# Last layer: the four query units in two pairs of seven block products, and ScalarE squaring the expanded keys

## The chip, the core and the metric

The kernel runs on one core of a Trainium2 chip. TensorE multiplies matrices, VectorE and GpSimd do elementwise work, ScalarE computes activations and copies, and SyncE issues the DMAs. The metric is the device time of one launch in microseconds, as the median of several runs. All arithmetic is in float32.

## The reference

A sequence of 256 tokens with 1024 features passes a first block (a gated delta mixer, a mixture of experts, a small extra gate) and then two layers. The change touches only the last of these, which is attention with an index that chooses 64 keys per query:

```
def odd_layer(x, g_norm, w_in, g_kv, w_uk, w_uv, g_q, g_k, w_out, rel_bias):
    xn = rmsnorm(x, g_norm)
    q, ckv, qi, ki, wi, z = _split(xn @ w_in, ODD_SPLITS)   # q: 256 x 1024, 16 heads of 64
    q = rmsnorm(q.reshape(hd), g_q)
    ckv = rmsnorm(ckv, g_kv)
    k = rmsnorm((ckv @ w_uk).reshape(hd), g_k)
    v = (ckv @ w_uv).reshape(hd)
    ...
        score = einsum('bqh,bqhs->bqs', wib, relu(einsum('bqhd,bsd->bqhs', qib, ki)))
        _, idx = lax.top_k(score, top_k)                     # causal, 64 of 256
        logits = einsum('bqhd,bqkhd->bqhk', qb, ksel) * 64 ** -0.5 + bias
        probs = softmax(logits)
        out = einsum('bqhk,bqkhd->bqhd', probs, vsel)
    return x + (out * silu(z)) @ w_out
```

## The kernel before

Each engine has its own program, written out in order in `odd_tensor`, `odd_scalar`, `odd_vector`, `odd_gpsimd` and `odd_sync`; what binds them are semaphores. An engine never overtakes a waiting instruction of its own. Weights arrive in units of 1024 rows by 256 columns (1 MB) in slots; slots 0 to 3 hold the four query units, slots 4 and 5 the two expansions (keys, values). `xt` holds the input turned, features on the partitions.

TensorE's order in this layer (`odd_tensor`): the index queries (L3776), bias rows, index keys (L3784), the compressed rows (L3793), the index scores (L3803). Then the stretch that the change rewrites (the calls from L3949 on): `queries(0)`, the turning of the compressed rows (L320), `queries(1)`, `query_sums(0)`, `expand(4, 0)` and `expand(4, 1)` (the keys, L3834), `queries(2)`, `query_sums(1)`, `queries(3)`, `query_sums(2)`, the turning of the keys by `turn_tensor` (L320), `query_sums(3)`, `expand(5, 0)` (the values), `logits(0)`, `expand(5, 1)`, `logits(1)`, `gates(0)` (L3846). From there on gates, logits, weights and values alternate until the output product (L3944).

One `queries(i)` is 16 matmuls of a 128x128 weight tile on 256 tokens (L3815); in the trace each float32 matmul has two records. The result stands in bank 2 or 3, features on the partitions. ScalarE's `keep_queries` copies it out, scaled, into `qT` (L4041) and squares it (L4042); `query_sums` adds the squares of each head by a matmul (L3825). ScalarE's `expand` copies the expanded keys out (L4047).

VectorE (`odd_vector`) makes the choice of keys: for each half t of the queries it weighs the scores (L4143, L4145), then finds the 64 largest in eight steps of MAX8 and MATCH_REPLACE8 (L4152, L4153), and writes the mask (L4155). After both halves it squares the expanded keys (L4161), adds the squares (L4162), and scales the keys by their norms, one instruction for each half of the tokens (L4165), for which ScalarE computes Ln and Exp (L4091, L4093). GpSimd adds the mask to the bias, four instructions for each half (L4347), each half from the moment that its mask is there.

## Time and profile before

| | |
|---|---|
| median of 3 runs | 1010.59 us (1009.43 to 1010.63) |
| profiled execution, its own time | 1010.96 us |
| its span in the trace | 1009.6 us |
| TensorE busy | 964.8 us (96%) |
| VectorE busy | 556.2 us (55%) |
| ScalarE busy | 335.3 us (33%) |
| GpSimd busy | 52.5 us (5%) |

The span is the time from the first to the last instruction in the trace; the launch takes 1.4 us more. The table says that TensorE is nearly always busy; where it isn't, and which stretch another engine decides, only the rows by time say. In a row of a timeline, the first number is the start in us from the beginning of the span, the second the time that the group of instructions took, and the bracket at the end how long the engine was idle before it and which instruction ended that.

### The profile page before, as it was taken

To read this page: it belongs to the slowest core of one execution; us is meant where nothing else is said; L and a number is where in the kernel's file an instruction comes from. 1 tells how busy PE (TensorE), PEld (TensorE's weight loads), DVE (VectorE), ACT (ScalarE), POOL (GpSimd) and SP (SyncE) were. 2 spreads that over 40 slices of the span, in tenths; PEclk is the share of its full clock that TensorE was granted. 3 is DMA by queue.
4 is the path that set the end of the run, shared out by engine and by line. 5 is a ranking of instruction groups with operands and counts; after the bars stand their busy time and mean duration, and the time that the engine had idled before them with its cause. 6 is when DMAs were issued, how large, how long until landed. Compare 5 with 4: busy or idle time off the path is not lost.

```text
span 1009.6 us, 21951 instructions
## 1 busy us (share of the span) xinstructions
PE 964.8 (96%) x9305; PEld 750.0 (74%) x9305; DVE 556.2 (55%) x1192; ACT 335.3 (33%) x904; POOL 52.5 (5%) x81
## 2 busy tenths in 40 slices
PE   9999999999999999799877999999999999999998
PEld 6788888888887794344322589988888988877887
DVE  3976876876868233111100496875555465194675
ACT  2455557556545222001100223132111321233550
POOL 1111011011000000000000000000000000034000
PEclk9999999999999999899987999999999999999999
DMA  8213215134156999999999934442555344652221
GB/s 347 87 65 133 102 65 178 56 136 180 45 187 268 423 372 354 423 429 427 436 429 411 407 162 149 169 176 90 186 182 179 127 168 167 185 192 84 84 84 43
DMA packets 34311, 211.63 MB, mean 210 GB/s; under 512 B 4432, under 2 KB 8976, under 8 KB 15904
## 3 DMA queue, kind: packets, MB, share of 16 engines
q1 hardware_dynamic: 33920, 210.13, 54.0%
q8 instruction: 76, 1.25, 0.5%
q14 instruction: 27, 0.22, 0.1%
q10 hardware_dynamic: 288, 0.03, 0.0%
HBM read 209.03 MB, written 1.11 MB: 208 GB/s over the span
## 4 chain that ended last, share of the span: by engine, by line
PE 81%; DMA 7%; DVE 4%; SPq 3%; issue 2%; ACT 2%; POOL 0%; DVEq 0%; ACTq 0%; POOLq 0%
PE ps L558 11%; PE ps L3174 9%; PE ps L3074 5%; DMA slots<-in_w 5%; PE ps L584 5%; PE ps L2036 3%; PE ps L3846 3%; PE ps L2920 3%; PE ps L3815 3%; SPq L1922 3%; PE ps L3944 2%; PE ps L970 2%; PE ps L3214 2%; PE ps L2684 2%; PE ps L2007 2%
## 5 line engine op out<-in xcount | busy, mean ns | idle before, releaser
L558 PE MATMUL ps<-xt,slots 128*128 128x256 f32 x512 | 122.3, 384 | 0.0
L558 PEld LDWEIGHTS ps<-xt,slots 128*128 128x128 f32 x512 | 93.8, 190 | 12.8 <-issue 0.4
L1308 DVE SCALAR_TENSOR_TENSOR arena<-arena 128x256 f32<-128x256 f32 x128 | 56.6, 501 | 0.0
L2036 PE MATMUL ps<-arena 128*32 128x512 f32 x224 | 47.5, 639 | 6.7 <-DMA arena<-in_w 6.1
L2378 DVE TENSOR_TENSOR arena<-arena,ps 128x256 f32<-128x256 f32 x8 | 3.4, 421 | 87.9 <-ACT arena L2168 87.9
L2036 PE MATMUL ps<-slots,arena 128*32 128x512 f32 x192 | 47.6, 641 | 2.4 <-DMA xt<-in_wu 2.4
L4347 POOL TENSOR_TENSOR arena<-arena 128x512 f32<-128x512 f32 (+1 forms) x8 | 17.8, 2262 | 597.3 <-DVE arena L4155 597.3
L2168 ACT ACTIVATE arena<-ps 128x256 f32<-128x256 f32 x8 | 3.1, 384 | 111.6 <-PE ps L2036 111.6
L970 PE MATMUL ps<-slots,yt 128*128 128x256 f32 x128 | 30.3, 396 | 2.1 <-DMA slots<-in_wu 2.1
L2036 PEld LDWEIGHTS ps<-arena 128*32 128x32 f32 x224 | 11.9, 117 | 26.4 <-issue 19.3
L3846 PE MATMUL ps<-xt,slots 128*128 128x256 f32 x128 | 30.6, 385 | 0.6 <-ACT arena L4047 0.6
L2007 PE MATMUL ps<-arena,x 128*128 128x128 f32 x256 | 30.4, 276 | 0.1
L2007 PEld LDWEIGHTS ps<-arena,x 128*128 128x128 f32 x256 | 29.3, 192 | 1.3 <-issue 0.8
L3174 PE MATMUL ps<-slots,yt 128*128 128x256 f32 x128 | 30.2, 379 | 0.0
L3174 PE MATMUL ps<-extra,arena 128*128 128x256 f32 x128 | 30.2, 379 | 0.0
L3174 PE MATMUL ps<-slots,arena 128*128 128x256 f32 x128 | 30.2, 379 | 0.0
L970 PEld LDWEIGHTS ps<-slots,yt 128*128 128x128 f32 x128 | 24.9, 197 | 6.0 <-issue 2.5
L3815 PE MATMUL ps<-xt,slots 128*128 128x256 f32 x128 | 28.5, 380 | 0.0
L2388 DVE COPY arena<-ps 128x512 f32<-128x512 f32 x7 | 4.8, 692 | 40.8 <-PE ps L2076 40.8
L3815 PEld LDWEIGHTS ps<-xt,slots 128*128 128x128 f32 x128 | 24.1, 190 | 3.9 <-issue 0.8
L3846 PEld LDWEIGHTS ps<-xt,slots 128*128 128x128 f32 x128 | 23.2, 190 | 4.9 <-issue 2.0
L3174 PEld LDWEIGHTS ps<-extra,arena 128*128 128x128 f32 x128 | 24.3, 190 | 3.3
(590 smaller groups left out, 2178.8 us busy)
## 6 DMA issues: line engine op xcount, KB each, us to landing
slots<-in_wu SPq DMA_DIRECT2D x90, 1024.0 KB, 5.7
arena<-in_wu SPq DMA_DIRECT2D x20, 1024.0 KB, 12.9
arena<-in_w SPq DMA_DIRECT2D x5, 4096.0 KB, 27.9
slots<-in_w SPq DMA_DIRECT2D x8, 2048.0 KB, 33.0
extra<-in_w SPq DMA_DIRECT2D x2, 4096.0 KB, 28.6
yt<-in_w SPq DMA_DIRECT2D x3, 2048.0 KB, 29.4
extra<-in_wu SPq DMA_DIRECT2D x4, 1024.0 KB, 19.7
xt<-in_wu SPq DMA_DIRECT2D x4, 1024.0 KB, 30.3
```

The source lines that it names most:

```text
L558: q = M.matmul(bank(b, T), self.slots[:, s, k, n * P:(n + 1) * P], self.xt[:, k, :], start=(k == 0), stop=(k == KT - 1))
L584: q = M.matmul(bank(b, UC), rows[:, k, :], weights[:, k, :], start=(k == 0), stop=(k == HK - 1))
L970: q = M.matmul(self.out_bank(t, cg), self.yt[:, KT + k, t * P:(t + 1) * P], self.slots[:, s, k, :], start=(k == 0 and (cg % 2 == 0 or (t, ...
L1308: q = V.scalar_tensor_tensor(g.cn[:, s], src, w, g.cn[:, s], ALU.mult, ALU.add)
L1922: SP.dma_start(part(self.flat(s)), part(I["wu"][U_MOE + u].rearrange("p a b -> p (a b)"))).then_inc(*(self.lands(s) if b else g.low_in.up()))
L2007: q = M.matmul(g.gathered_in(i, k), self.x[:, t, k * P:(k + 1) * P], g.sb[:, t].rearrange("p e s -> p (e s)"), start=(t == 0), stop=(t == ...
L2036: q = M.matmul(self.ps[r, 2, :], g.xg[:, half * (KT // 2) + k, r], self.flat(slots[e])[:, k * 512:(k + 1) * 512], start=(half == 0 and k = ...
L2920: q = M.matmul(into[:, n * P:(n + 1) * P], w[:, k, n * P:(n + 1) * P], x[:, k, :], start=(n == 0 and k == 0 and not more), stop=(k == HK - ...
L3074: q = M.matmul(into[n], rows[:, k, :], weights[:, k, :], start=(h == 1 and k == 0 and n in (1, 5, 6, 7)), stop=(h == 0 and k == HK - 1), s ...
L3174: q = M.matmul(into, rows[:, k, :], weights[:, k, :], start=(k == 0 and not more), stop=(k == HK - 1), skip_group_check=True)
L3815: q = M.matmul(bank(2 + i % 2, T, n * T), self.slots[:, i, k, n * P:(n + 1) * P], self.xt[:, k, :], start=(k == 0), stop=(k == KT - 1), sk ...
L3846: q = M.matmul(bank(g.z_banks[u], T, n * T), self.slots[:, u, k, n * P:(n + 1) * P], self.xt[:, k, :], start=(n == 0 and k == 0), stop=(k ...
```

## The change

The product of queries is a product of two matrices. Two units side by side (slots 0 and 1, then 2 and 3) are cut in two by rows and in two by units, and the tokens in two halves, so that a pair of units is a 2x2 by 2x2 block product. It is made from seven block products in place of eight, by sums and differences of blocks made beforehand and folds made afterwards. One block product is 8 matmuls of a 128x128 tile on 128 tokens. `query_product(p, n)` is product n (1, 7, 2, 6, 5, 4, 3 in this order) of pair p. Products 2, 4 and 3 add onto what 1, 7 and 5 have left in banks 0, 3 and 2; before that ScalarE has to copy product 1 (`keep_query_first`) and VectorE has to use 7 and 5.

VectorE gets: four operations on the token blocks (`mix_query_rows`, 128x512: y11-y21, s1=y21+y22, s2=s1-y11, y12-s2, with y for blocks of `xt`), four on the weights of each pair (`mix_queries`, 128x1024: t1=b12-b11, b22-b12 in place of b12, t2=b22-t1, t4=b21-t2, with b for blocks of the two slots), and five folds for each pair (`fold_queries`, 256 elements a partition). The folds are numbered through: `q_folds` 1 to 5 for the first pair, 6 to 10 for the second. Folds 1 and 2 of the first pair stand between the two searches, 3 to 5 behind the weighing of the second half; folds 6 and 7 stand between the two scalings of the keys, 8 to 10 behind them.

ScalarE scales and squares the queries in three parts for each pair (`keep_query`), two of them from `qT` in SBUF. It squares the expanded keys out of the banks itself (in `expand`), and VectorE's squaring (L4161) goes. On TensorE the query sums stand together in pairs, and the turning of the keys is parted: two turns ahead of `expand(5, 0)`, two behind.

```diff
+        def query_product(p, n):
+            a, b = 2 * p, 2 * p + 1
+            one, two, rows, xt = self.slots[:, a], self.slots[:, b], g.q_rows, self.xt
+            t1, t2, t4 = g.q_mixes[p]
+            if n == 1:
+                g.q_in.append([self.landing(s) for s in (a, b)])
+                M.wait_ge(*g.q_in[p][0])
+                if p == 0:
+                    M.wait_ge(*g.rrow_kept(1))
+                else:
+                    M.wait_ge(*g.expand_kept(1))
+            elif n == 7:
+                M.wait_ge(*g.q_rows_made(1))
+                M.wait_ge(*g.q_mix(4 * p + 2))
+                if p > 0:
+                    M.wait_ge(*g.q_folds(5))
+            elif n == 2:
+                M.wait_ge(*g.q_first(p + 1))
+            elif n == 6:
+                M.wait_ge(*g.q_rows_made(3))
+                M.wait_ge(*g.q_mix(4 * p + 3))
+            elif n == 5:
+                M.wait_ge(*g.q_mix(4 * p + 1))
+            elif n == 4:
+                M.wait_ge(*g.q_mix(4 * p + 4))
+                M.wait_ge(*g.q_folds(5 * p + 2))
+            else:
+                M.wait_ge(*g.q_in[p][1])
+                M.wait_ge(*g.q_rows_made(4))
+                M.wait_ge(*g.q_folds(5 * p + 3))
+            into = bank({1: 0, 2: 0, 6: 1, 5: 2, 3: 2, 7: 3, 4: 3}[n], T)
+            x, w = {1: (xt[:, 0:HK, 0:P], one[:, 0:HK]), 2: (xt[:, HK:KT, 0:P], one[:, HK:KT]), 6: (rows[:, 1], t2),
+                    7: (rows[:, 2], two[:, 0:HK]), 5: (rows[:, 0], t1), 4: (xt[:, HK:KT, P:2 * P], t4),
+                    3: (rows[:, 3], two[:, HK:KT])}[n]
+            for f in range(2):
+                for k in range(HK):
+                    q = M.matmul(into[:, f * P:(f + 1) * P], w[:, k, f * P:(f + 1) * P], x[:, k, :],
+                                 start=(f == 0 and k == 0 and n not in (2, 3, 4)), stop=(k == HK - 1),
+                                 skip_group_check=True)
+            if n == 4:
+                q.then_inc(*self.multiplied[a].up())
+            elif n == 3:
+                q.then_inc(*self.multiplied[b].up())
+                g.q_pair_done.append([self.multiplied[s].last() for s in (a, b)])
...
-        queries(0)
+        for n in (1, 7, 2, 6):
+            query_product(0, n)
         M.wait_ge(*g.relu(2))
         M.wait_ge(*g.c_norm(1))
         self.turn_tensor(g.ck, 2, [4], g.c_turned, g.c_cols)
-        queries(1)
-        query_sums(0)
+        for n in (5, 4, 3):
+            query_product(0, n)
         M.wait_ge(*g.c_cols(1))
         M.wait_ge(*self.landing(4))
         expand(4, 0)
         expand(4, 1)
-        queries(2)
+        query_sums(0)
         query_sums(1)
-        queries(3)
-        query_sums(2)
+        for n in (1, 7, 2, 6, 5, 4, 3):
+            query_product(1, n)
         M.wait_ge(*g.expand_kept(2))
         M.wait_ge(*g.scaled(1))
-        self.turn_tensor(g.kk, KT, [4, 5], g.k_turned, g.k_kept)
-        query_sums(3)
+        turn_keys(0)
+        turn_keys(1)
+        M.wait_ge(*g.q_folds(10))
         M.wait_ge(*self.landing(5))
         expand(5, 0)
+        turn_keys(2)
+        turn_keys(3)
+        query_sums(2)
+        query_sums(3)
         logits(0)
...
+        def keep_query_first(p):
+            A.wait_ge(*g.q_of(p, 1))
+            if p > 0:
+                A.wait_ge(*g.q_folds(5))
+            A.activation(g.q_sums_of[0], bank(0, T), ACT.Copy).then_inc(*g.q_first.up())
+        def keep_query(p, part):
+            a, scale = 4 * p, g.feat[:, F_Q:F_Q + 1]
+            if part == 0:
+                A.wait_ge(*g.q_of(p, 2))
+                at, src = (slice(a, a + 2), slice(0, P)), bank(0, T).rearrange("p (n t) -> p n t", n=2)
+            elif part == 1:
+                A.wait_ge(*g.q_folds(5 * p + 4))
+                at = (slice(a, a + 4), slice(P, T))
+            else:
+                A.wait_ge(*g.q_folds(5 * p + 5))
+                at = (slice(a + 2, a + 4), slice(0, P))
+            if part > 0:
+                src = g.qT[:, at[0], at[1]]
+            A.activation(g.q_squares[:, at[0], at[1]], src, ACT.Square).then_inc(*g.q_squared.up())
+            if part > 0:
+                A.wait_ge(*g.q_squared.last())
+            q = A.activation(g.qT[:, at[0], at[1]], src, ACT.Copy, scale=scale)
+            if part == 2:
+                q.then_inc(*g.q_kept.up())
...
+            if s == 4:
+                A.activation(halves(g.pq[:, 0, t]), self.ps[:, b0:b0 + 2], ACT.Square)
+            A.activation(halves(dst[:, t]), self.ps[:, b0:b0 + 2], ACT.Copy).then_inc(*g.expand_kept.up())
...
-        keep_queries(0)
+        keep_query_first(0)
+        keep_query(0, 0)
         self.turn_scalar(g.ckt, 2, [4], g.c_turned, g.c_cols, g.fcol(F_KV))
-        keep_queries(1)
+        keep_query(0, 1)
+        keep_query(0, 2)
         expand(4, 0, g.kk)
         expand(4, 1, g.kk)
-        keep_queries(2)
+        keep_query_first(1)
         A.wait_ge(*g.squares(1))
         A.activation(g.sh[:, :, :], g.sh[:, :, :], ACT.Ln, scale=1.0 / CD, bias=self.col(0)).then_inc(*g.s_ln.up())
         A.wait_ge(*g.s_ln(1))
         A.activation(g.sh[:, :, :], g.sh[:, :, :], ACT.Exp, scale=-0.5).then_inc(*g.s_exp.up())
-        keep_queries(3)
-        self.turn_scalar(g.kT, KT, [4, 5], g.k_turned, g.k_kept, lambda k: g.feat[:, F_K:F_K + 1])
+        keep_query(1, 0)
+        turn_keys(0)
+        turn_keys(1)
+        keep_query(1, 1)
+        keep_query(1, 2)
+        expand(5, 0, g.vv)
+        turn_keys(2)
+        turn_keys(3)
         A.wait_ge(*g.q_sums(4))
...
+        def fold_queries(p, n):
+            u1, u2, u3 = g.q_sums_of
+            first, second, third, fourth = (bank(m, T) for m in range(4))
+            pair = lambda a: a.rearrange("p (n t) -> p n t", n=2)
+            low, high = (g.qT[:, 4 * p + 2 * m:4 * p + 2 * m + 2, :] for m in range(2))
+            if n == 0:
+                V.wait_ge(*g.q_first(p + 1))
+                V.wait_ge(*g.q_of(p, 6))
+                o = V.tensor_tensor(u2, u1, second, ALU.add)
+            elif n == 1:
+                V.wait_ge(*g.q_folds(5 * p + 1))
+                o = V.tensor_tensor(u3, u2, fourth, ALU.add)
+            elif n == 2:
+                V.wait_ge(*g.q_of(p, 5))
+                V.wait_ge(*g.q_folds(5 * p + 2))
+                o = V.tensor_tensor(high[:, :, P:T], pair(u3), pair(third), ALU.add)
+            elif n == 3:
+                V.wait_ge(*g.q_pair_done[p][0])
+                o = V.tensor_tensor(low[:, :, P:T], pair(u2), pair(fourth), ALU.add)
+            else:
+                V.wait_ge(*g.q_pair_done[p][1])
+                o = V.tensor_tensor(high[:, :, 0:P], pair(u2), pair(third), ALU.add)
+            o.then_inc(*g.q_folds.up())
...
+        mix_query_rows()
+        mix_queries(0)
         V.wait_ge(*g.index_kept(1))
         V.wait_ge(*g.r_spread(1))
         V.tensor_tensor(g.kit[:, :], g.kit[:, :], bank(0, T), ALU.mult).then_inc(*g.kit_made.up())
+        mix_queries(1)
         for t in range(NT):
             S = (t + 1) * P
             V.wait_ge(*g.wi_kept(t + 1))
...
                     v(q)
             q.then_inc(*g.masked.up())
             V.wait_ge(*g.masked(2 * t + 1))
+            if t > 0:
+                for n in (2, 3, 4):
+                    fold_queries(0, n)
             v(V.tensor_tensor(wk, mk, g.late[:, t, 0:S], ALU.subtract))
             for r in range(SEL // 8):
                 v(V.max(g.best[:, :], wk))
                 v(V.match_replace(wk, g.best[:, :], wk, TAKEN))
             v(V.tensor_scalar(wk, wk, TAKEN / 2, -BIG, ALU.is_gt, ALU.mult))
             V.tensor_tensor(mk, wk, g.late[:, t, 0:S], ALU.subtract).then_inc(*g.masked.up())
+            if t == 0:
+                fold_queries(0, 0)
+                fold_queries(0, 1)
 
         byh = lambda x: x.rearrange("p (h d) -> p h d", h=CH)
         squares = g.pq[:, 0].rearrange("p t (h d) -> p t h d", h=CH)
         V.wait_ge(*g.expand_kept(2))
         keys = g.kk[:, :, :].rearrange("p t (h d) -> p t h d", h=CH)
-        v(V.tensor_tensor(squares, keys, keys, ALU.mult))
         V.tensor_reduce(g.sh[:, :, :], squares, AX, ALU.add).then_inc(*g.squares.up())
         V.wait_ge(*g.s_exp(1))
         for t in range(NT):
             q = V.tensor_tensor(keys[:, t], keys[:, t], g.sh[:, t].unsqueeze(2).to_broadcast([P, CH, CD]), ALU.mult)
+            if t == 0:
+                fold_queries(1, 0)
+                fold_queries(1, 1)
         q.then_inc(*g.scaled.up())
+        for n in (2, 3, 4):
+            fold_queries(1, n)
```

On TensorE, from the index scores to the second pair, this stands before (the last column is the shape of the result, then the number of matmuls):

```order
L3803 MATMUL ps<-arena 128x256 x4
L3815 MATMUL ps<-xt,slots 128x256 x16
L320 MATMUL ps<-cst,arena 128x128 x4
L3815 MATMUL ps<-xt,slots 128x256 x16
L3825 MATMUL ps<-cst,arena 128x2 x4
L3834 MATMUL ps<-slots,arena 128x512 x8
L3815 MATMUL ps<-xt,slots 128x256 x16
L3825 MATMUL ps<-cst,arena 128x2 x4
L3815 MATMUL ps<-xt,slots 128x256 x16
L3825 MATMUL ps<-cst,arena 128x2 x4
L320 MATMUL ps<-cst,arena 128x128 x16
```

and this after, where L3857 is `query_product` (the first four rows are products 1, 7, 2, 6 of pair 0), L3892 the expansion and L3883 the query sums:

```order
L3814 MATMUL ps<-arena 128x256 x4
L3857 MATMUL ps<-xt,slots 128x128 x8
L3857 MATMUL ps<-arena,slots 128x128 x8
L3857 MATMUL ps<-xt,slots 128x128 x8
L3857 MATMUL ps<-arena 128x128 x8
L320 MATMUL ps<-cst,arena 128x128 x4
L3857 MATMUL ps<-arena 128x128 x8
L3857 MATMUL ps<-xt,arena 128x128 x8
L3857 MATMUL ps<-arena,slots 128x128 x8
L3892 MATMUL ps<-slots,arena 128x512 x8
L3883 MATMUL ps<-cst,arena 128x2 x8
L3857 MATMUL ps<-xt,slots 128x128 x8
```

Both query units of the first pair now stand ahead of the expansion of the keys in 56 small matmuls in place of 32 large ones, and the query sums of the first pair behind it.

On VectorE, between the end of the first search and the second one, this stands before:

```order
L4154 TENSOR_SCALAR arena<-arena 128x128
L4155 TENSOR_TENSOR arena<-arena 128x128
L4143 TENSOR_SCALAR arena<-arena 128x256
L4145 SCALAR_TENSOR_TENSOR arena<-arena 128x256 x3
L4150 TENSOR_TENSOR arena<-arena 128x256
L4152 MAX arena<-arena 128x8
```

and this after (L4273 to L4286 are folds 1 to 5 of the first pair):

```order
L4314 TENSOR_SCALAR arena<-arena 128x128
L4315 TENSOR_TENSOR arena<-arena 128x128
L4273 TENSOR_TENSOR arena<-arena,ps 128x256
L4276 TENSOR_TENSOR arena<-arena,ps 128x256
L4300 TENSOR_SCALAR arena<-arena 128x256
L4302 SCALAR_TENSOR_TENSOR arena<-arena 128x256 x3
L4280 TENSOR_TENSOR yt<-arena,ps 128x2x128
L4283 TENSOR_TENSOR yt<-arena,ps 128x2x128
L4286 TENSOR_TENSOR yt<-arena,ps 128x2x128
L4310 TENSOR_TENSOR arena<-arena 128x256
L4312 MAX arena<-arena 128x8
```

Two folds have come ahead of the weighing of the second half and three behind it, ahead of its search.

## Rows read from the trace of the kernel before

**Rows 1.** Chain of waits, last layer: start us, us, what.
```profile
883.59 7.10 PE ps L3815 x32
890.70 0.44 PE ps L320 x4
891.13 6.91 PE ps L3815 x32
898.04 0.79 PE ps L3825 x8
898.83 6.97 PE ps L3834 x16
...
921.30 0.51 PE ps L320 x4
...
921.83 1.58 ACT yt L334 x4
...
923.45 0.66 PE ps L320 x4
...
932.75 1.03 ACT arena L4047
...
933.92 5.42 PE ps L3846 x24
```

**Rows 2.** TensorE by time, layer before: start us, us, engine, line, operation, count.
```profile
642.39 1.95 PE L2920 MATMUL ps<-arena,slots 128*128 128x128 f32 x16
644.17 1.95 PE L2920 MATMUL ps<-yt,slots 128*128 128x128 f32 x16
```

**Rows 3.** ScalarE by time, last layer.
```profile
888.12 0.91 ACT L4035 ACTIVATE arena<-arena 128x256 f32<-128x256 f32 x2
...
898.08 0.69 ACT L4041 ACTIVATE yt<-ps,arena 128x512 f32<-128x512 f32 x1 [5.44 <-PE ps L3815]
898.67 0.59 ACT L4042 ACTIVATE arena<-ps 128x512 f32<-128x512 f32 x1
...
921.83 3.15 ACT L334 ACTIVATE yt<-ps,arena 128x256 f32<-128x256 f32 x8
```

**Rows 4.** VectorE by time, layer before.
```profile
642.59 0.42 DVE L3400 TENSOR_TENSOR arena<-arena,ps 128x256 f32<-128x256 f32 x1 [0.23 <-PE ps L2920]
...
645.85 1.22 DVE L3376 TENSOR_TENSOR arena<-slots,arena 128x1024 f32<-128x1024 f32 x1
```

**Rows 5.** VectorE by time, last layer, before the first search.
```profile
874.82 0.42 DVE L4137 TENSOR_TENSOR arena<-arena,ps 128x256 f32<-128x256 f32 x1 [7.58 <-ACT arena L4004]
883.65 0.29 DVE L4143 TENSOR_SCALAR arena<-arena 128x128 f32<-128x128 f32 x1 [8.41 <-ACT arena L4020]
```

**Rows 6.** DMA queue by time, then DMA issues: KB each, median us to landing.
```profile
859.79 2.05 SPq L276 DMA_DIRECT2D slots<-in_wu  x2
...
slots<-in_wu SPq DMA_DIRECT2D x2, 1024.0 KB, 6.0
```

**Rows 7.** VectorE and then GpSimd by time, last layer.
```profile
892.08 4.24 DVE L4145 SCALAR_TENSOR_TENSOR arena<-arena 128x256 f32<-128x256 f32 x3
...
906.90 4.09 DVE L4161 TENSOR_TENSOR arena<-arena 128x2048 f32<-128x2048 f32 x1 [0.49 <-ACT arena L4047]
911.02 2.29 DVE L4162 TENSOR_REDUCE arena<-arena 128x32 f32<-128x2048 f32 x1
914.43 5.47 DVE L4165 TENSOR_TENSOR arena<-arena 128x1024 f32<-128x1024 f32 x2 [1.12 <-ACT arena L4093]
...
891.92 5.52 POOL L4347 TENSOR_TENSOR arena<-arena 128x512 f32<-128x512 f32 x4 [588.24 <-DVE arena L4155]
906.48 12.33 POOL L4347 TENSOR_TENSOR arena<-arena 128x1024 f32<-128x1024 f32 x4 [9.04 <-DVE arena L4155]
```

**Rows 8.** TensorE by time, experts; then busy us by window, the granted clock behind POOL.
```profile
494.49 0.62 PE L2036 MATMUL ps<-slots,arena 128*32 128x512 f32 x2 [2.39 <-DMA xt<-in_wu]
...
496.00:497.00 1.00, 1.00 (x8) 0.27 (x4) 0.00 (x0) 0.00 (x0) 0.00 (x0) 0.50 0.91 393
```

More of the change, by code:

```diff
@@ L3805, in odd_tensor @@
             q.then_inc(*g.scores.up())
-        g.q_done, g.z_done = [], []
-        def queries(i):
-            M.wait_ge(*self.landing(i))
-            if i > 1:
-                M.wait_ge(*g.q_kept(i - 1))
-            for n in range(2):
-                for k in range(KT):
-                    q = M.matmul(bank(2 + i % 2, T, n * T), self.slots[:, i, k, n * P:(n + 1) * P], self.xt[:, k, :],
-                                 start=(k == 0), stop=(k == KT - 1), skip_group_check=True)
-            q.then_inc(*self.multiplied[i].up())
-            g.q_done.append(self.multiplied[i].last())
+        g.q_in, g.q_pair_done, g.z_done = [], [], []
@@ new lines, in odd_tensor @@
+        HK = KT // 2
+        def query_product(p, n):
[43 more added lines that the diff above has]
+            else:
+                q.then_inc(*g.q_products.up())
@@ L3820, in query_sums, with turn_keys @@
+        def turn_keys(j):
+            if j > 1:
+                M.wait_ge(*g.k_kept(j - 1))
+            for f in range(2):
+                for t in range(NT):
+                    q = M.transpose(bank(4 + j % 2, P, (2 * f + t) * P), g.kk[:, t, (2 * j + f) * P:(2 * j + f + 1) * P],
+                                    c["ident"])
+            q.then_inc(*g.k_turned.up())
         def query_sums(i):
-            M.wait_ge(*g.q_kept(i + 1))
+            M.wait_ge(*g.q_kept(i // 2 + 1))
             for n in range(2):
```

51 lines of the change are left out of this document (42 added, 9 removed).

## The prediction

> **What bounds the kernel now.** The table of busy shares comes first: TensorE is busy 96% of the span. That alone would say that fewer matmul columns are less time, so the next view is the chain of waits in the last layer. Up to the gates at 933.92 every piece of it but a few is TensorE's own work [rows 1]: two of the four query blocks (there are four such, 7.10 and 6.91 us in turn) with the turning of the compressed rows between them, the query sums, the expansion of the keys. Two pieces are ScalarE's: 1.58 us in the turning of the keys (921.83) and 1.03 us ahead of the gates (932.75). Behind 933.92 nothing is changed, TensorE works without a wait of its own, and what starts later there ends later. So the whole question is at what time the gates start. The views after that are the timelines of ScalarE, VectorE and GpSimd beside this stretch, since the new products wait for folds and copies on them.
>
> **What it removes.** Four blocks of 7.10 and 6.91 us, twice each, are 28.0 us [rows 1]. In their place come 14 block products of 16 records on 128 columns. The layer before has products of exactly this form: they start 1.78 us apart, and the last result is there 1.95 us after the start [rows 2]. 14 x 1.78 = 24.9 us, so TensorE's own work shrinks by 3.1 us, a ninth and not an eighth. The turning of the keys took from 921.30 to 924.11, 2.8 us, with the wait for ScalarE in it [rows 1]. Parted in two, with the expansion of the values between, it waits for nothing and costs four times 0.44 us (the 4 records at 890.70 [rows 1]), 1.8 us. That is another 1.0 us. Together: -4.1 us. The rest of TensorE's work (turning of the compressed rows, expansions, sums, logits) is the same and only stands in another order.
>
> **VectorE's mixing lies in idle time.** Before the operation at 874.82 it is idle for 7.58 us, and before 883.65 for 8.41 us [rows 5]. The four operations on tokens (half of 1.22 us and a little, 2.6 us) and the four on the first pair of weights (1.22 us each, started some 1.15 us apart [rows 4], 4.7 us) fill 7.3 of the first 7.58 us, the four on the second pair 4.7 of the second 8.41 us. The last two query units are issued from 859.79 on and land 6.0 us after (median), 868 at the latest [rows 6], ahead of both. Should the first set overrun by a microsecond, the operation at 874.82 has until TensorE's scores at 882.0, so I cost it at nothing; were a unit to land 8 us late, the cover would be gone and each microsecond would count.
>
> **The waits that come in**, one by one, with the start of the first product at 883.59:
>
> First wait, product 2. Products 1 and 7 are issued by 883.59 + 3.56 = 887.15. Product 2 adds onto bank 0, which ScalarE must copy first, and ScalarE is in its chain for the compressed rows until 888.12 + 0.91 = 889.03 [rows 3]. The old `keep_queries(0)` also waited for that, but TensorE had 7 us of `queries(0)` to issue meanwhile and now has 3.6. A copy of 256 elements takes 0.39 us (3.15 us for 8 [rows 3]), and TensorE starts 0.14 us after what it waits for (933.92 against 932.75 + 1.03 [rows 1]): product 2 at 889.56. Loss 2.4 us.
>
> Second wait, product 3 of the first pair. Products 2, 6, the turning, 5 and 4 are issued by 889.56 + 4 x 1.78 + 0.44 = 897.12. Fold 1 needs product 6, there at 891.34 + 1.95 = 893.3, though VectorE is free from 891.8 on; folds 1 and 2 at 0.42 us each [rows 4] end at 894.2, the first weighing at 894.5. Then come the three operations at L4145, which took 4.24 us while GpSimd worked from 891.92 to 897.4 [rows 7], 1.41 us each against 0.42 for an operation of this size alone [rows 4]. The same GpSimd work now slows two of them: 894.5 + 2 x 1.4 + 0.5 = 897.8, fold 3 at 898.2, product 3 at 898.35. Loss 1.2 us.
>
> Third wait, product 3 of the second pair. TensorE: 898.35 + 1.78 + 6.97 (keys) + 2 x 0.79 (sums) + 6 x 1.78 = 919.4. VectorE: product 3 is there at 900.3, fold 5 at 900.75. The search took from 896.32 to 906.41 (end of L4145, start of the idle 0.49 us before 906.90 [rows 7]); its first operation had GpSimd beside it and now hasn't, so I take 9.2 us: 909.95. The squaring of 4.09 us is gone, which is why this isn't worse; the sums take 2.29 [rows 7], ScalarE's Ln and Exp 0.65 (two small ones of about 0.3), the first scaling half of 5.47 [rows 7]: 915.6. Fold 6 waits for product 6, there at 916.0; folds 6 and 7 end at 916.85, the second scaling at 919.6, fold 8 at 920.0, and product 3 starts at 920.2. Loss 0.8 us.
>
> Fourth wait, logits. TensorE: 920.2 + 1.78 + 2 x 0.44 + 3.54 (the later expansion is half of 6.97 and a little) + 2 x 0.44 + 2 x 0.79 = 928.85. ScalarE: it turns out the first keys by 924.2, then squares and scales the last query parts (0.59 and 0.69 [rows 3], then about 0.4 and 0.4, with two waits on itself: 2.3 us), copies the values (1.03 [rows 1]) and turns out the other keys (4 x 0.39 [rows 3]): 929.1. Loss 0.4 us.
>
> **The sum.** -3.1 - 1.0 + 2.4 + 1.2 + 0.8 + 0.4 = +0.7; with some 0.1 for the first matmuls behind a wait, +0.8 us. The profiled execution took 1010.96 us (span 1009.6) and would take 1011.8; the median is 0.37 us lower, which is within the scatter of the three runs, so the forecast is 1010.59 + 0.8 = 1011.4 us.
>
> **What the trace of before doesn't show.** (a) How much GpSimd slows the weighing and the scalings in their new places: at best not at all (0.42 and 1.22 us), which takes 1.9 us from the second and third wait together and gives -1.1 in all; at worst every one as now, +1.5. I take the middle since the same GpSimd work stands there. (b) Folds while GpSimd works: 0.42 us each if they run as [rows 4], 1.41 us each if they are slowed as L4145 is; I take 0.42, because the sums of squares at 911.02, with one operand, kept to 2.29 us beside GpSimd [rows 7]. (c) The clock after the first wait: below.
>
> That VectorE and GpSimd hinder each other stands in rows 7. The Trainium skill (GPSIMD Engine Reference, Specifications) says that this happens with VectorE instructions with two inputs in SBUF or in a two-port mode. A fold has one input in the banks, so by that rule it is not slowed and the sum stays.
>
> **Rivals.**
>
> *The clock falls in the first wait.* TensorE is without work from 887.3 to 889.56, 2.3 us. Among the experts it was idle for 2.39 us before 494.49, and the granted clock at 496 was 0.50, which is 1.2 in place of 2.4 GHz [rows 8]. For it: nearly the same idle time. Against it: among the experts only a small part of the array worked (128*32 in that row), here TensorE works in full on both sides of the wait. Between half of product 2 and both products 2 and 6 would run at half speed, 0.9 to 3.6 us longer; I take 1.7. The weighing then starts later and meets less of GpSimd's work, so that 0.7 to 1.2 us remain: 1012.3 us.
>
> The Trainium skill (TensorE: Matmul & The Clock Gate, Why this matters for your kernels) warns of idle gaps above some 3 us. By that this wait would be free and the sum would stay at 1011.4; the 2.39 us of rows 8 speak against it.
>
> *The folds are slowed by GpSimd* (slower). GpSimd works on the second mask for 12.3 us [rows 7], from 909.9 on, so folds 6, 7 and 8 are all beside it, and folds 1 and 2 beside the first mask. Each fold between product 6 and the freeing of its bank is on TensorE's path. At 1.41 us each, 1.0 us more, times five, and the search shifted too: some +5 to +7 us, 1016 to 1018. It decides from 0.6 us a fold on, where the five cost 1 us more and the kernel is slower by 2. For it: rows 7. Against it: the one-operand sums.
>
> *The waits are shorter than reckoned* (faster). If the weighings run alone and ScalarE copies product 1 in between, the 4.1 us are kept to 3: 1007.8. Against it: ScalarE's order is fixed, and 889.03 is a measured time. The likelier form is -1 us by (a): 1009.5, no change.
>
> *It doesn't do what it says:* a pair's mixes late by a landing, so that scores start late. Rows 6 leave 2 us at least; 1014.
>
> **Chances.** What a measurement of this kernel can tell from no change is about 0.2%, 2.0 us. Forecast with the clock kept 0.45 (1011.4), with the clock down 0.25 (1012.3), waits shorter 0.15 (1009.5, a third of it below 1008.6), folds slowed 0.11 (mostly above 1012.6), late mixes or something else 0.04. From these: faster 0.05, same 0.79, slower 0.16 (0.10 of the folds, 0.03 of the clock with more slowing, 0.03 others). The range 1009.3 to 1013.4 takes in both ends of (a) with the clock down, and leaves out the folds' 1016 and the 1007.8.
>
> **What would show it.** Product rows 1.78 us apart: the first term. TensorE idle for about 2.3 us ahead of product 2, released by ScalarE; about 1 us ahead of each product 3, released by VectorE; the gates' start near 934.7 (933.92 before). A granted clock of 0.50 behind this wait is the first rival. Folds of over 0.6 us are the second. A start of the scores later than 882.0 means that the mixing wasn't hidden. The forecast is wrong if the gates start before 932.7 or after 936.

## The result, and the profile after

The changed kernel took 1012.09 us (median of 17 runs, 1010.58 to 1014.02), against 1010.59 us for the kernel before on the same chip (17 runs, 1009.08 to 1012.13). The ratio is 1.0016, with a 95% interval of 1.0009 to 1.0024: slower by 1.6 us (1.5 between the medians), within the 0.2% that were called no change, and 0.7 us above the forecast of 1011.4.

The forecast was made at the start of the gates, so the comparison begins there. "Stretch" below is the time from the start of the first query product to the start of the gates. It leaves out what differs between two executions further up: TensorE's clock falls among the experts in every profile of this study, not always at the same places, and the stretch starts anywhere from 881.5 to 883.5 us. Before, it began at 883.52 by TensorE's timeline (the chain has 883.59) and ended at 933.92 [rows 1], 50.40 us:

```profile
883.52 7.17 PE L3815 MATMUL ps<-xt,slots 128*128 128x256 f32 x32
```

After, it is TensorE's timeline below (start, time taken, engine, line, operation, tiles, shape; in the bracket the idle time before and what ended it; the last line of such a view counts only the records up to the time at which the view stops):

```profile
880.56 1.58 PE L3814 MATMUL ps<-arena 64*128 64x128 f32 x16 [0.68 <-issue]
882.07 2.05 PE L3857 MATMUL ps<-xt,slots 128*128 128x128 f32 x16
...
887.90 3.68 PE L3857 MATMUL ps<-xt,slots 128*128 128x128 f32 x16 [1.99 <-ACT arena L4106]
891.40 1.97 PE L3857 MATMUL ps<-arena 128*128 128x128 f32 x16
...
895.42 1.95 PE L3857 MATMUL ps<-xt,arena 128*128 128x128 f32 x16
897.74 2.02 PE L3857 MATMUL ps<-arena,slots 128*128 128x128 f32 x16 [0.36 <-DVE yt L4280]
...
918.97 1.95 PE L3857 MATMUL ps<-arena,slots 128*128 128x128 f32 x16
...
921.63 3.60 PE L3892 MATMUL ps<-slots,arena 128*128 128x512 f32 x8
925.07 1.04 PE L3874 MATMUL ps<-cst,arena 128*128 128x128 f32 x8
925.94 1.84 PE L3883 MATMUL ps<-cst,arena 128*128 128x2 f32 x16
927.89 0.72 PE L3921 MATMUL ps<-yt 64*128 64x128 f32 x8
928.54 5.40 PE L3892 MATMUL ps<-slots,arena 128*128 128x512 f32 x8
933.87 0.71 PE L3921 MATMUL ps<-yt 64*128 64x128 f32 x8
935.14 2.18 PE L3904 MATMUL ps<-xt,slots 128*128 128x256 f32 x9 [0.56 <-ACT arena L4135]
```

The reader is to see three things. Products run 1.78 us apart (1.86 to 1.89 behind a wait or another kind of work), and the wait for ScalarE's copy ahead of product 2 is there (1.99 us idle, 2.16 us from the time at which it could have been issued). Two groups take nearly twice their time: product 2 with 3.68 us in place of 2.05, and the later expansion of the values (L3892) with 5.40 us, where the same form took 3.60 at 921.63. And no wait stands ahead of the second pair's product 3 at 918.97. The stretch is 882.07 to 935.14, 53.07 us, 2.67 longer than before.

The view by windows says what slowed the two groups (bounds, length, busy time with the count for PE, PEld, DVE, ACT, POOL; then the granted clock, the DMA share and GB/s):

```profile
886.00:888.00 2.00, 0.10 (x1) 0.10 (x1) 1.79 (x9) 1.78 (x6) 0.00 (x0) 1.00 0.99 418
888.00:890.00 2.00, 2.00 (x10) 2.00 (x11) 1.83 (x9) 0.00 (x0) 0.00 (x0) 0.50 0.41 172
890.00:892.00 2.00, 2.00 (x14) 2.00 (x14) 0.29 (x1) 0.38 (x2) 1.53 (x2) 0.64 0.00 0
...
929.00:931.00 2.00, 2.00 (x4) 0.79 (x3) 1.69 (x6) 0.00 (x0) 0.00 (x0) 0.50 0.00 0
931.00:933.00 2.00, 2.00 (x5) 0.82 (x4) 0.00 (x0) 0.00 (x0) 0.00 (x0) 0.65 0.00 0
```

The granted clock was 0.50, the lower of TensorE's two levels (1.2 in place of 2.4 GHz), behind the first wait and again behind the query sums and logits. In the profile of before it stayed at 1.00 through the whole stretch:

```profile
883.50:934.00 50.50, 49.37 (x231) 37.03 (x230) 35.59 (x75) 17.70 (x43) 17.85 (x8) 1.00 0.39 138
```

VectorE's side (columns as in TensorE's timeline), with the mixing first, then the first pair's folds, then the second's:

```profile
865.71 0.69 DVE L4244 TENSOR_TENSOR arena<-xt 128x512 f32<-128x512 f32 x1
...
871.89 1.23 DVE L4262 TENSOR_TENSOR arena<-slots,arena 128x1024 f32<-128x1024 f32 x1
873.37 0.42 DVE L4293 TENSOR_TENSOR arena<-arena,ps 128x256 f32<-128x256 f32 x1 [0.25 <-ACT arena L4067]
...
893.47 0.42 DVE L4273 TENSOR_TENSOR arena<-arena,ps 128x256 f32<-128x256 f32 x1 [3.15 <-PE ps L3857]
...
894.27 1.31 DVE L4300 TENSOR_SCALAR arena<-arena 128x256 f32<-128x256 f32 x1
895.61 1.53 DVE L4302 SCALAR_TENSOR_TENSOR arena<-arena 128x256 f32<-128x256 f32 x3
897.17 0.42 DVE L4280 TENSOR_TENSOR yt<-arena,ps 128x256 f32<-128x256 f32 x1
...
912.08 2.99 DVE L4327 TENSOR_TENSOR arena<-arena 128x1024 f32<-128x1024 f32 x1 [0.65 <-ACT arena L4190]
...
916.46 1.91 DVE L4327 TENSOR_TENSOR arena<-arena 128x1024 f32<-128x1024 f32 x1
918.29 0.41 DVE L4280 TENSOR_TENSOR yt<-arena,ps 128x256 f32<-128x256 f32 x1
```

After the mixing VectorE still waits 0.25 us for ScalarE where it was idle for 7.58 us [rows 5]: the cover was just wide enough. Every fold takes 0.42 us, those beside GpSimd too, which worked on the second mask from 909.31 on:

```profile
909.31 11.28 POOL L4514 TENSOR_TENSOR arena<-arena 128x1024 f32<-128x1024 f32 x4 [13.89 <-DVE arena L4315]
```

### The profile page after: what moved, and what is told of

The parts are those of the page before. It is cut to its first block, busy times and chain, and to the rows that moved or that the text cites. A ratio compares the mean times of both kernels' runs of the same rounds, so it can differ in the third digit from the quotient of the medians.

```text
span 1010.8 us, 22188 instructions
## 1 busy us (share of the span) xinstructions
PE 963.5 (95%) x9401; PEld 753.0 (74%) x9401; DVE 564.4 (56%) x1213; ACT 339.4 (34%) x912; POOL 51.1 (5%) x81
## 4 chain that ended last, share of the span: by engine, by line
PE 81%; DMA 6%; DVE 5%; SPq 3%; ACT 2%; issue 2%; POOL 0%; DVEq 0%; ACTq 0%; POOLq 0%
PE ps L558 11%; PE ps L3174 9%; PE ps L3074 5%; PE ps L584 5%; DMA arena<-in_w 4%; PE ps L2036 4%; PE ps L3904 3%; PE ps L2920 3%; SPq L1922 2%; PE ps L4002 2%; PE ps L970 2%; PE ps L3214 2%; PE ps L2007 2%; PE ps L3857 2%; PE ps L2684 2%
## 5 line engine op out<-in xcount | busy, mean ns | idle before, releaser
L558 PE MATMUL ps<-xt,slots 128*128 128x256 f32 x512 | 122.3, 384 | 0.0
L558 PEld LDWEIGHTS ps<-xt,slots 128*128 128x128 f32 x512 | 93.8, 190 | 12.8 <-issue 0.4
L2036 PE MATMUL ps<-slots,arena 128*32 128x512 f32 x192 | 45.1, 613 | 1.0 <-DMA xt<-in_wu 0.8
L3904 PE MATMUL ps<-xt,slots 128*128 128x256 f32 x128 | 30.6, 385 | 0.6 <-ACT arena L4135 0.6
L970 PEld LDWEIGHTS ps<-slots,yt 128*128 128x128 f32 x128 | 23.9, 190 | 5.6 <-issue 2.6
L3904 PEld LDWEIGHTS ps<-xt,slots 128*128 128x128 f32 x128 | 23.2, 190 | 4.9 <-issue 2.0
L3174 PEld LDWEIGHTS ps<-slots,arena 128*128 128x128 f32 x128 | 24.3, 190 | 3.3
L3174 PEld LDWEIGHTS ps<-slots,yt 128*128 128x128 f32 x128 | 24.2, 190 | 3.3
```

Of the source, the lines that this page charges most:

```text
L558: q = M.matmul(bank(b, T), self.slots[:, s, k, n * P:(n + 1) * P], self.xt[:, k, :], start=(k == 0), stop=(k == KT - 1))
L970: q = M.matmul(self.out_bank(t, cg), self.yt[:, KT + k, t * P:(t + 1) * P], self.slots[:, s, k, :], start=(k == 0 and (cg % 2 == 0 or (t, ...
L2036: q = M.matmul(self.ps[r, 2, :], g.xg[:, half * (KT // 2) + k, r], self.flat(slots[e])[:, k * 512:(k + 1) * 512], start=(half == 0 and k = ...
L3174: q = M.matmul(into, rows[:, k, :], weights[:, k, :], start=(k == 0 and not more), stop=(k == HK - 1), skip_group_check=True)
L3904: q = M.matmul(bank(g.z_banks[u], T, n * T), self.slots[:, u, k, n * P:(n + 1) * P], self.xt[:, k, :], start=(n == 0 and k == 0), stop=(k ...
```

## The experiments

Theory A: the change would be even or a little slower by its waits, and what it lost beyond that are the two clock falls. Theory B: the loss is in the waits and in VectorE's added work themselves; the clock only shows it.

**The first wait filled.** Five matmuls of 256 columns, whose result isn't used, stand in the wait.

```diff
-        for n in (1, 7, 2, 6):
+        for n in (1, 7):
+            query_product(0, n)
+        for k in range(5):
+            M.matmul(bank(1, T), self.slots[:, 0, k, 0:P], self.xt[:, k, :], start=(k == 0), stop=(k == 4),
+                     skip_group_check=True)
+        for n in (2, 6):
             query_product(0, n)
```

> The changed kernel with five more matmuls of 256 columns (2.2 us) between products 7 and 2 of the first pair, into a bank that product 6 then overwrites: the wait for ScalarE stays where it is, but TensorE works through it. Theory A (half of the loss is the clock that falls behind this wait): no granted clock of 0.50 behind 887, products 2 and 6 take 3.6 us together and not 5.5, the gates start 0.7 to 1.7 us earlier after the start of the first product than the 53.1 us of the changed kernel, ratio to the kernel before 1.0005 to 1.001. Theory B (the waits alone cost the time, the clock is made up for by the later wait of product 3): ratio stays 1.0016.

Measured: ratio to before 0.9999 (0.999 to 1.0008), 1010.53 us. TensorE around the filler and at the end of the stretch:

```profile
887.08 2.32 PE L4009 MATMUL ps<-xt,slots 128*128 128x256 f32 x10
889.24 2.05 PE L3857 MATMUL ps<-xt,slots 128*128 128x128 f32 x16
...
898.42 1.80 PE L3857 MATMUL ps<-arena,slots 128*128 128x128 f32 x14 [1.33 <-DVE yt L4285]
...
928.58 0.71 PE L3921 MATMUL ps<-yt 64*128 64x128 f32 x8
929.22 3.70 PE L3892 MATMUL ps<-slots,arena 128*128 128x512 f32 x8
932.85 0.72 PE L3921 MATMUL ps<-yt 64*128 64x128 f32 x8
934.13 3.04 PE L3904 MATMUL ps<-xt,slots 128*128 128x256 f32 x13 [0.56 <-ACT arena L4140]
```

Product 2 starts at the same distance from the first product as before the filling (5.83 us), but takes 2.05 us, and the clock falls nowhere in this layer. The stretch is 50.72 us, 0.32 more than the kernel before and 2.35 less than the changed one. So the waits and the added work cost what the forecast's sum gave, nearly, and the rest was the clock. It also shows that the first fall hangs on TensorE being idle, not on what stands behind the wait. The ratio came out below theory A's 1.0005 to 1.001, and the stretch gained 2.35 us in place of 0.7 to 1.7, because the second fall was missing too. That isn't the filler's doing as far as is shown: two kernels below are without the second fall though nothing there was changed.

**The waits taken away.** Products in the order 1, 7, 6, 5, 2, 4, 3, and fold 3 (which product 3 waits for) right behind folds 1 and 2, ahead of the second half's weighing.

```diff
-        for n in (1, 7, 2, 6):
+        for n in (1, 7, 6, 5, 2):
             query_product(0, n)
...
-        for n in (5, 4, 3):
+        for n in (4, 3):
             query_product(0, n)
...
             if t > 0:
-                for n in (2, 3, 4):
+                for n in (3, 4):
                     fold_queries(0, n)
...
                 fold_queries(0, 1)
+                fold_queries(0, 2)
```

(The second pair likewise.)

> The changed kernel with the products in the order 1, 7, 6, 5, 2, 4, 3 in both pairs, and the third fold of each pair beside the first two (between the searches; between the scalings). Theory A (the loss is the wait for ScalarE's copy of product 1, the clock behind it and product 3's wait for the fold): TensorE has 7.1 us of products before it needs the copy, none of these waits is left, the first pair ends 2.5 to 3.5 us earlier, ratio to the kernel before 0.997 to 0.999 (1007.5 to 1009.5 us). Theory B (VectorE's chain of weighing, search, sums and scaling sets the gates' start in the end): the gain goes into a wait of product 3 of the second pair or of the keys' turning for VectorE, and the ratio is 0.9995 to 1.001.

Measured: 0.9957 (0.9943 to 0.997), 1006.26 us. TensorE from the first product:

```profile
883.42 2.05 PE L3857 MATMUL ps<-xt,slots 128*128 128x128 f32 x16
885.31 1.95 PE L3857 MATMUL ps<-arena,slots 128*128 128x128 f32 x16
887.09 3.74 PE L3857 MATMUL ps<-arena 128*128 128x128 f32 x32
890.67 1.95 PE L3857 MATMUL ps<-xt,slots 128*128 128x128 f32 x16
892.45 0.60 PE L320 MATMUL ps<-cst,arena 128*128 128x128 f32 x4
892.89 1.95 PE L3857 MATMUL ps<-xt,arena 128*128 128x128 f32 x16
894.68 1.95 PE L3857 MATMUL ps<-arena,slots 128*128 128x128 f32 x16
...
925.49 5.39 PE L3892 MATMUL ps<-slots,arena 128*128 128x512 f32 x8
```

No bracket is left among the products. The stretch is 48.68 us, with one fall in it (the expansion at 925.49); without that fall, which costs 5.39 - 3.70 = 1.7 us, it would be 47.0, 3.7 us below the filled kernel, where the two waits that are gone measure 2.16 and 1.50 us. The same 14 products that made the kernel slower by 1.6 us make it faster by 4.3 us (3.0 to 5.8) once nothing is waited for. This version beats both kernels, and by more than theory A's 0.997 to 0.999.

**Only fold 3 put back** behind the weighing, with the new order of the products kept.

```diff
-                for n in (3, 4):
+                for n in (2, 3, 4):
                     fold_queries(0, n)
```

(In the second pair likewise.)

> The order 1, 7, 6, 5, 2, 4, 3 with the folds where the changed kernel has them. Theory A (the order alone takes away the wait for ScalarE, but fold 3 then lies behind the weighing of the second half, which GpSimd slows): product 3 of the first pair waits 1 to 2.5 us for fold 3, ratio 0.997 to 0.9985, stretch 49.5 to 50.5 us without a fall of the clock. Theory B (the place of the folds doesn't matter since VectorE is ahead): ratio 0.9957 as with the early fold.

Measured: 1.0016 (1.0004 to 1.0028), 1011.85 us. VectorE, then TensorE:

```profile
890.44 0.87 DVE L4300 TENSOR_SCALAR arena<-arena 128x256 f32<-128x256 f32 x1
891.35 4.20 DVE L4302 SCALAR_TENSOR_TENSOR arena<-arena 128x256 f32<-128x256 f32 x3
895.58 0.42 DVE L4280 TENSOR_TENSOR yt<-arena,ps 128x256 f32<-128x256 f32 x1
```

```profile
896.14 3.65 PE L3857 MATMUL ps<-arena,slots 128*128 128x128 f32 x16 [3.25 <-DVE yt L4280]
```

The whole gain is gone; the stretch is 52.00 us. Fold 3 stands behind a weighing that GpSimd slows to 4.20 us, as in [rows 7], product 3 waits 3.25 us, and the clock falls behind that wait too (3.65 us for a product in place of 1.95). Theory A named the right cause but priced it too low: it had a wait of 1 to 2.5 us, no fall, and a ratio of 0.997 to 0.9985. In the second pair product 3 doesn't wait, so it is the place of one operation of 0.42 us in the first pair that decides between 1006 and 1012 us.

**The narrow matmuls parted.** In the kernel with its first wait unfilled, half of `expand(5, 0)` goes between the turning of the keys and the query sums, and ScalarE copies the values later.

```diff
-        expand(5, 0)
+        expand(5, 0, (0,))
         turn_keys(2)
         turn_keys(3)
+        expand(5, 0, (1,))
         query_sums(2)
```

> The changed kernel with the first expansion of the values cut in its two halves of 1.7 us, the later two turnings of the keys between them, and ScalarE's copy of the values behind the turned keys. Theory A (the clock fell at 929 because query sums of 2 columns, a short wait and logits on 64 rows follow each other with too little work in them): with one turning less beside them the fall becomes rarer, the second expansion of the values takes 3.6 us and not 5.3, ratio 1.0005 to 1.001, if it doesn't fall in the profile. Theory B (the fall at 929 is a matter of one execution, or has another cause): ratio stays 1.0016, and the profile may show it again.

Measured: 1.0007 (0.9998 to 1.0016), 1011.53 us; stretch 51.19 us. The fall behind the first wait is there (at 890.6), the one at the end isn't. With one fall the stretch stands 0.47 us above the filled kernel's and 1.88 below the changed kernel's, so the second fall is the dearer; some 0.2 us of that is the parting itself (see the next run). The timed ratios overlap, so this kernel alone doesn't prove it.

**Both edits together** (new order, early fold 3, parted narrow matmuls).

> The order 1, 7, 6, 5, 2, 4, 3 with the third fold early, and the values' first expansion cut in two with the keys' turnings between. In the profile of the first of these alone the clock fell once more, at 925.5, and the second expansion of the values took 5.4 us instead of 3.7. Theory A (the fall comes of too little work in a row behind the turnings): both together have no fall in this layer, the stretch from the first product to the gates is 47.0 to 47.4 us (48.7 with the order alone), ratio to the kernel before 0.994 to 0.9955. Theory B (cutting the expansion does nothing): a fall again, 48.7 us, ratio as the order alone, 0.9957.

Measured: 0.996 (0.9946 to 0.9974), 1006.82 us; stretch 46.80 us with no fall in it, 1.9 less than with the order alone and 0.2 less than that without its fall. It is 3.6 us below the kernel before, which is what the forecast's first term gives by measured rows (-2.6) with the keys' turning (-1.0): with no wait left, nothing else remains. But the ratio isn't the 0.994 to 0.9955 of theory A: the medians don't differ (1006.26 and 1006.82, five runs each). The profile of the order alone was its slowest execution, 1009.13 us with a mean granted clock of 0.983; the other four took 1005.98 to 1007.10 us with 0.985 to 0.988. One profile is one execution, and its fall is not the rule there.

**Only ScalarE's squares** (the products of before, with the squaring on ScalarE):

```diff
+            if s == 4:
+                A.activation(halves(g.pq[:, 0, t]), self.ps[:, b0:b0 + 2], ACT.Square)
...
-        v(V.tensor_tensor(squares, keys, keys, ALU.mult))
```

(Against the kernel before.)

> The kernel before with one part of the change alone: ScalarE squares the expanded keys from the banks, VectorE's squaring of 4.1 us is left out. Theory A (the keys' scaling wasn't what the turning waited for, it ended 1.4 us ahead of it): ratio 0.9995 to 1.0005. Theory B (GpSimd and VectorE hindered each other there, and what stands behind comes earlier): ratio 0.998 to 0.9995.

Measured: 0.999 (0.998 to 1.0), 1009.62 us; stretch 50.39 against 50.40. GpSimd's second mask and VectorE's scaling get quicker:

```profile
905.37 9.28 POOL L4348 TENSOR_TENSOR arena<-arena 128x1024 f32<-128x1024 f32 x4 [9.04 <-DVE arena L4157]
```

```profile
913.31 3.55 DVE L4166 TENSOR_TENSOR arena<-arena 128x1024 f32<-128x1024 f32 x2 [4.32 <-ACT arena L4095]
```

12.33 us became 9.28 and 5.47 became 3.55 [rows 7]: there is no squaring beside GpSimd any more, and the scaling, which waits for ScalarE until 913.31, overlaps it only up to 914.65. But TensorE's chain sets the end here. The ratio lies in theory B's range, though its interval reaches 1.0; what was quicker didn't come through to the gates, so in the stretch theory A holds. This part of the change frees VectorE for the second pair's folds; alone it moves the stretch by nothing.

**The mixing all but left out.** Every mixing operation works on 4 columns, so the queries aren't the products asked for.

```diff
-            rows = g.q_rows
+            y11, y12, y21, y22 = (y[:, :, 0:4] for y in (y11, y12, y21, y22))
+            rows = g.q_rows[:, :, :, 0:4]
...
+            b11, b21, b12, b22, t1, t2, t4 = (y[:, :, 0:4] for y in (b11, b21, b12, b22, t1, t2, t4))
```

> The changed kernel with VectorE's mixing of tokens and weights reduced to 4 of 128 or 256 columns (the rest of the blocks is left out, so the queries are not the reference's). Theory A (the mixing of 7.5 and 4.9 us lies wholly in time in which VectorE was idle): the scores start as before in relation to the last matmul ahead of them, and the stretch from the first product to the gates is as in the changed kernel for the same falls of the clock, 50.7 us without one, 53.1 with two. Theory B (mixing costs): the stretch or the gap ahead of the scores (0.68 us) is shorter by 0.5 us or more.

Measured: 1010.06 us, one run; stretch 51.39 us with the fall behind the first wait alone, 0.2 from the parted kernel with the same single fall, and what the filled kernel's +0.32 and the first fall's 0.65 (reckoned below) give together: 51.37. The gap ahead of the scores is 0.67 us, 0.68 with the full mixing. The mixing was hidden.

**The narrow matmuls tripled**, in the filled kernel: 16 more matmuls with 2 columns (32 records) ahead of the 8 of the last query sums, to the same result.

```diff
         turn_keys(3)
+        for more in range(2):
+            for i in (2, 3):
+                M.wait_ge(*g.q_kept(2))
+                for n in range(2):
+                    for t in range(NT):
+                        M.matmul(bank(6, 2, t * CH + 4 * i + 2 * n), g.q_squares[:, 2 * i + n, t * P:(t + 1) * P],
+                                 c["columns"][:, 6:8], start=True, stop=True, skip_group_check=True)
         query_sums(2)
```

> The changed kernel with the filled first wait, and the 8 query sums of the second pair (matmuls with 2 columns) made three times over, the first two times for nothing. TensorE is busy in the trace all through. Theory A (matmuls of 2 columns don't keep the clock up): 3.4 us more of them, and a fall of the clock to 0.50 behind them, the second expansion of the values takes 5.3 us and not 3.7; the stretch is 50.7 + 3.4 + 1.7 = 55.8 us. Theory B (what the trace shows as busy keeps the clock up): no fall, stretch 54.1 us.

Measured: 1016.3 us, one run; stretch 57.36 us. The windows:

```profile
928.00:930.00 2.00, 2.00 (x20) 2.00 (x19) 0.00 (x0) 0.00 (x0) 0.00 (x0) 0.94 0.04 8
930.00:932.00 2.00, 2.00 (x14) 1.98 (x14) 0.00 (x0) 0.67 (x3) 0.00 (x0) 0.50 0.00 0
932.00:934.00 2.00, 2.00 (x6) 0.90 (x5) 1.50 (x5) 0.00 (x0) 0.00 (x0) 0.50 0.00 0
934.00:936.00 2.00, 2.00 (x4) 0.81 (x3) 0.48 (x2) 0.00 (x0) 0.00 (x0) 0.50 0.00 0
```

TensorE is busy 2.00 of 2.00 us in each, and still the clock falls to 0.50, for about 6.8 us. The stretch is 6.64 us longer than the filled kernel's, of which 3.50 are the added matmuls; the fall cost the other 3.1, more than the 1.7 of theory A, whose stretch was 55.8.

**The control: as much work, but wide.** In the filled kernel, in the same place, 8 matmuls of 256 columns. This run was on another chip, where the kernel before took 1010.09 us (one run).

```diff
         turn_keys(3)
+        M.wait_ge(*g.q_kept(2))
+        for k in range(8):
+            M.matmul(bank(1, T), self.slots[:, 5, k, 0:P], self.xt[:, k, :], start=(k == 0), stop=(k == 7),
+                     skip_group_check=True)
         query_sums(2)
```

> This is the kernel with the filled first wait, and 8 more matmuls of 256 columns on 128 features stand on TensorE between the turning of the last keys and the query sums; their result is not used. They are the control for the kernel with more narrow matmuls in the same place, whose clock fell for 6.8 us. Theory A (the clock falls in the second place because the cluster of matmuls with 2 columns counts for little): wide matmuls in front leave the same narrow cluster behind them as in the filled kernel, which kept 1.00, so the granted clock stays at 1.00 and the stretch from the start of the first product to the start of the gates is that of the filled kernel and 8 x 0.44 = 3.5 us, 50.7 + 3.5 = 54.2 us. Theory B (any longer stay in this place, or any work put there, brings the fall): a fall to 0.50 behind them, at least 1.7 us more, 56 us or more.

Measured: 1014.47 us, one run; stretch 883.44 to 937.43, 53.99 us against the 54.2 of theory A.

```profile
928.00:930.00 2.00, 2.00 (x11) 1.77 (x10) 0.00 (x0) 0.45 (x2) 0.00 (x0) 1.00 0.00 0
930.00:932.00 2.00, 2.00 (x20) 1.96 (x20) 0.00 (x0) 0.02 (x1) 0.00 (x0) 1.00 0.00 0
932.00:934.00 2.00, 2.00 (x12) 1.16 (x13) 1.15 (x5) 0.65 (x3) 0.00 (x0) 1.00 0.00 0
```

The same 3.5 us of added work brings no fall when it is wide. That speaks for what is multiplied, and against the time spent or the place, as what took the clock. Each of these two is one execution, and falls come and go between executions, so it is strong evidence and no proof; the fall in the narrow one is the longest in this layer of any profile here.

**What the timed runs add.** The record has the mean granted clock of each timed execution, over the whole kernel. It is 0.9832 in the changed kernel (mean of 17 runs) and 0.9854 in the kernel before (27 runs made with the later experiments); the filled kernel has 0.9851, the parted one 0.9841, the late fold 0.9843 (11 runs each), the new order alone and with the parting 0.9860 (5 each). The difference of 0.0022 is 2.2 us of full clock in 1011; in the changed kernel's profile the two falls together take 3.4 us of it (windows of 1 us from 888 to 892 and from 928 to 933). So, as an estimate that takes the falls among the experts as alike in both kernels, a timed execution of the changed kernel loses on average some two thirds of what its profile shows, and one of the new order next to nothing.

## Why the prediction was right, and where not

The time was held by the range, and the main mechanism was the one forecast: gain on TensorE given back in waits. What the clock added on top was foreseen in part, as a rival, and in part not at all. Term by term, with the filled kernel as the one without clock falls:

- **Products, -3.1 us**: measured -2.6. The 14 products took 12.77 and 12.59 us, 25.4 and not 24.9: four of them, each the first behind a wait or another kind of work, held the next up for 1.86 to 1.89 us and not 1.78. **Keys' turning, -1.0**: four times 0.44 us, as reckoned.
- **First wait, +2.4**: 2.16. It came about as described; in the changed kernel ScalarE's chain ended at 886.67 + 0.91 = 887.58, 5.51 us behind the first product, against 5.44 reckoned from [rows 3].
- **Second wait, +1.2**: 1.50 in the filled kernel, 0.54 in the changed one, where TensorE was late already.
- **Third wait, +0.8**: nothing. The second scaling was reckoned at half of 5.47 us and took 1.91, so that in the changed kernel fold 8 ended at 918.70, ahead of 918.97. **Fourth wait, +0.4**: 0.25. From the last query sums to the logits 1.95 us pass, where the first pair's sums pass the engine on after 1.70; ScalarE's last keys are copied at 927.75, and the logits start 0.14 us later, as forecast.
- **The sum, +0.8**: +0.32 without a fall. The waits came to 3.9 us and not 4.8, the products gave back 0.5 less: small errors of both signs.
- **The mixing at nothing**: right (0.25 us of idle time left behind it, and the run almost without it).
- **Rival "the clock falls in the first wait" (0.25)**: it happened in the profile. Product 2 lost 1.61 us by it, and the second wait took 0.96 of that back, so 0.65 us remain; the prediction had said 0.7 to 1.2. It gave this rival 1012.3, which is nearer to the 1012.09 measured than the forecast is. The Trainium skill (TensorE: Matmul & The Clock Gate, Why this matters for your kernels) warns of idle gaps above some 3 us, and by that this wait was free; here 1.99 us were enough, in the profiles of all three kernels that had the wait (changed, parted, mixing left out: falls at 888.0, 890.6 and 888.8, that is 0.1 to 1.4 us after product 2 had started). The prediction gave this case too small a chance against the forecast.
- **What failed**: the step that priced everything behind the first wait at full clock. The later expansion of the values was put at half of 6.97 us, 3.54, and took 5.33 from start to start, 1.70 more than in the filled kernel. 0.32 + 0.65 + 1.70 = 2.67 us, the whole difference of the stretches. No case in the prediction had this second fall. That the change made it likelier is a reading, not shown: it moved the sums of two units, 16 records of 2 columns, next to the logits on 64 rows, where before 8 such records at a time stood between wider work. For it speak the tripled kernel and its wide control. But of five profiles with this group as the change has it (changed, new order, filled, late fold, mixing left out) two have the fall and three not, and the same 16 records behind the keys' expansion (906.47) never lost the clock. What decides in one execution stays open.
- **So the median lay 0.7 us above the forecast through the clock.** By the sum with measured rows the kernel would have stood at +0.3 us. With two thirds of the profile's 0.65 and 1.70 us on top (the estimate from the mean clocks) it is +1.9, against the 1.6 measured. The nearness to the forecast is partly luck: its +0.8 was 0.5 too high for the waits and products, and the falls, one of which it didn't have at all, lay on the other side.
- **Rival "folds slowed"**: refuted, 0.42 us each beside GpSimd. The Trainium skill (GPSIMD Engine Reference, Specifications) names two inputs in SBUF or a two-port mode as the condition; the folds, with one input in the banks, agree.
- **Rival "waits shorter"**: true of the third wait; in all 0.9 us shorter, of which the products took back 0.5.

The time moved by 1.6 us (0.9 to 2.4), the profiled stretch by 2.67. The timed runs show no clock by stretch, so how often each of the two falls occurs stays open; that they come in part of the executions is what the mean clocks say.

## What to carry to other kernels

Fewer columns paid here only once what the new products wait for was done beforehand: look for each new wait's cheapest cure in the order of independent products and in the place of the small operation that frees the bank, before the arithmetic is judged. Here 4.3 us were to be had, and two orders of the same instructions stood 6 us apart. A wait on the bounding engine costs its own time and may cost nearly as much again in clock behind it (1.61 us behind one of 1.99 here), unless a later wait takes it back, as 0.96 of it was here. Work with few columns, gathered in one place, may do the same though the engine reads as busy. And a profile with a fall in it is to be held against the mean clock of the timed runs before its stretch is taken for the kernel's.

## What the runs showed of the hardware

- Idle time of 1.99 us on TensorE between full products was followed by a granted clock of 0.50 each time it occurred (three profiles), and so was idle time of 3.25 us (late fold); filled with 2.16 us of matmuls, it wasn't. A wait of 1.33 us never was followed by a fall (filled, wide and tripled kernels).
- Matmuls with 2 columns, without idle time, can be followed by a lower clock: 0.50 for about 6.8 us in the tripled kernel, none with wide ones in their place, one execution each. The group of 8 matmuls lost it in two profiles (changed, order alone) and kept it in the others with the same group (filled, late fold, mixing left out), so at that size it isn't certain.
- Beside GpSimd an operation on VectorE with one input could take longer too where that input and its output are in SBUF. The weighing's first (TENSOR_SCALAR, 256 elements) took 0.35 us in the kernel before, where it started ahead of GpSimd's work, and 0.35, 0.49, 0.87 and 1.31 in the new order, filled, late fold and changed kernels, where GpSimd was at work when it started. In each of these four it ended 0.15 or 0.16 us behind the GpSimd instruction that was running when it started (ends at 893.09, 894.32, 891.15 and 895.42), so it reads as waiting that one out, and its time depends on how much of that instruction was left. The sums of squares (TENSOR_REDUCE) took 2.28 to 2.29 us in every kernel, each time beside GpSimd.
- GpSimd's second mask took 12.33 us in the kernel before, 9.28 with ScalarE's squares alone and 11.3 in the changed kernel, by what VectorE did beside it, without cost to the end.
